# Forming the first pair's tokens already transposed, in a hybrid encoder kernel on one Trainium2 core

## The reference, cut to what matters

```python
def hier_moe(h, w_rg, b_rg, w_re, b_re, w_gate, w_up, w_down):
    t = h.reshape(B * S, D)
    ...                                   # group, two experts of it, weights
    for e in range(N_EXPERTS):            # 32
        he = jax.nn.silu(t @ w_gate[e]) * (t @ w_up[e])     # 1024 -> 256
        y = y + combine[:, e:e + 1] * (he @ w_down[e])      # 256 -> 1024
```

## Time and profile before

| | |
|---|---|
| median of 3 runs | 527.29 us (526.87 to 527.69) |
| profiled execution, span from first to last instruction | 526.4 us |
| profiled execution, its own time | not recorded apart from the span |
| PE busy | 491.7 us |
| PEld busy | 271.0 us |
| DVE, ACT, POOL busy | 212.8, 136.9, 75.1 us |
| packets of all DMAs | 139.95 MB, mean 266 GB/s |
| mean granted TensorE clock | 0.987 |

### The profile page before, as it was taken

One profiled execution on the slowest core, in us unless ns is written; L12 is line 12 of the kernel. 1 busy time (PEld: TensorE's weight loads), 2 busy tenths in 40 slices (PEclk: granted clock), 3 DMA queues, 4 the chain that ended last, 5 costly groups with the idle time before them and its releaser, 6 DMA issues.

```text
span 526.4 us, 7686 instructions
## 1 busy us (share of the span) xinstructions
PE 491.7 (93%) x2924; PEld 271.0 (51%) x2924; DVE 212.8 (40%) x565; ACT 136.9 (26%) x357; POOL 75.1 (14%) x101
## 2 busy tenths in 40 slices
PE   4999999999999999999999899999999978878894
PEld 4446544557765555455447555555555444444431
DVE  3317320666676671116763422223323312233167
ACT  3404211354476661203131111111111101112023
POOL 1000000361100000001113122222222222111000
PEclk9999999999999999999998999999999989999898
DMA  8996000010199004931089999999999999999984
GB/s 291 361 278 254 2 1 0 16 36 2 33 398 404 5 1 177 416 127 41 2 317 361 395 418 415 415 417 414 418 412 417 413 417 416 418 415 415 411 327 160
DMA packets 40134, 139.95 MB, mean 266 GB/s; under 512 B 9848, under 2 KB 12984, under 8 KB 31904
## 3 DMA queue, kind: packets, MB, share of 16 engines
q1 hardware_dynamic: 34752, 131.38, 63.5%
q0 software_dynamic: 4816, 7.85, 4.0%
q10 hardware_dynamic: 528, 0.22, 0.2%
HBM read 130.47 MB, written 16.39 MB: 279 GB/s over the span
## 4 chain that ended last, share of the span: by engine, by line
PE 65%; DMA 16%; SPq 9%; DVE 6%; issue 2%; ACT 1%; DVEq 0%; ACTq 0%; POOLq 0%
PE bank L747 12%; PE bank L1065 12%; DMA EW<-in_moe_w_up 9%; PE bank L933 9%; PE bank L1078 5%; SPq L615 5%; PE bank L906 5%; PE bank L976 3%; SPq L620 3%; PE bank L965 3%; DMA EW<-y_scratch 2%; PE bank L1038 2%; DMA EW<-in_w_in 2%; PE bank L755 1%; PE bank L853 1%
## 5 line engine op out<-in xcount | busy, mean ns | idle before, releaser
L1065 PE MATMUL bank<-EW,WO 128*64 128x256 f32 x640 | 78.5, 401 | 9.8 <-DMA EW<-in_moe_w_up 8.1
L1065 PEld LDWEIGHTS bank<-EW,WO 128*64 128x64 f32 x640 | 47.8, 144 | 35.6 <-DMA EW<-in_moe_w_up 9.8
L747 PE MATMUL bank<-EW,XT 128*128 128x512 f32 (+1 forms) x192 | 64.1, 495 | 0.0
L933 PE MATMUL bank<-WO,XT 128*128 128x512 f32 x128 | 56.6, 595 | 0.0
L1411 ACT ACTIVATE G<-bank 128x128 f32<-128x128 f32 x32 | 8.9, 277 | 178.9 <-PE bank L1065 178.9
L1778 DVE TENSOR_TENSOR G<-G,bank 128x128 f32<-128x128 f32 x32 | 9.2, 287 | 113.1 <-ACT G L1411 113.1
L2002 POOL DMA_INDIRECT y_scratch<-G,sidx x30 | 30.2, 1008 | 159.1 <-DVE G L1791 145.8
L747 PEld LDWEIGHTS bank<-EW,XT 128*128 128x128 f32 x192 | 32.9, 190 | 31.0 <-issue 31.0
L1791 DVE COPY G<-bank 128x512 f32<-128x512 f32 x32 | 22.1, 691 | 45.8 <-PE bank L1078 45.8
L1078 PE MATMUL bank<-EW,G 128*64 128x512 f32 x160 | 38.3, 599 | 0.0
L933 PEld LDWEIGHTS bank<-WO,XT 128*128 128x128 f32 x128 | 23.7, 190 | 27.3 <-issue 27.3
(11 more groups left out here) (295 smaller groups left out, 651.8 us busy)
## 6 DMA issues: line engine op xcount, KB each, us to landing
EW<-in_moe_w_gate SPq DMA_DIRECT2D x20, 1024.0 KB, 21.5
EW<-in_moe_w_up SPq DMA_DIRECT2D x20, 1024.0 KB, 21.4
EW<-in_moe_w_down SPq DMA_DIRECT2D x20, 1024.0 KB, 23.3
y_scratch<-MIX SPq DMA_DIRECT2D x8, 512.0 KB, 9.1
WO<-in_w_out SPq DMA_DIRECT2D x2, 2048.0 KB, 12.3
MIX<-in_moe_w_gate SPq DMA_DIRECT2D x4, 1024.0 KB, 20.6
MIX<-in_moe_w_up SPq DMA_DIRECT2D x4, 1024.0 KB, 22.6
WO<-in_moe_w_gate SPq DMA_DIRECT2D x4, 1024.0 KB, 19.7
```

The lines of the kernel that those rows point to most:

```text
L747: mm = pe.matmul(ps[:, 0:width], xnT[:, c, t * P:(t + 1) * P], w_in_sb[:, c, col:col + width], start=(c == 0), stop=(c == C - 1))
L933: mm = pe.matmul(ps[:, :], xnT[:, c, t * P:(t + 1) * P], w_out_sb[:, c, n * 512:(n + 1) * 512], start=(c == 0), stop=(c == C - 1))
L1065: mm = pe.matmul(bank[BLOCK * m:BLOCK * (m + 1), 0:2 * P].rearrange("p (w n) -> p w n", w=2), xeT[:, c, par * BLOCK:(par + 1) * BLOCK], wv ...
```

## The change

Pair 0's `pick` uses the rows of `X` as the stationary operand, in eight pieces of every eighth column, and `sel0` as the moving one, so that its products come out transposed, in the layout of the former transposes. For each t there are eight products with 128 columns, in place of two with 512. The copies to `xg[0]`, their semaphores and the eight transposes are gone: DVE and ACT copy from the banks to `xeT` with the gain as soon as bank 0 and bank 1 are complete. `pick_done` becomes `xe_full` 2 for SP and POOL. Pair 2's numbers move behind expert 0's `gate_up` on PE, and on DVE the weights of the last tile and `held_w` move ahead of pair 2's part.

```diff
-            sp.wait_ge(pick_done, 1)
+            sp.wait_ge(xe_full, 2)
...
-                    for n in range(2):
-                        mm = pe.matmul(banks[n][:, :], sel0[:, t].rearrange("p e s -> p (e s)"),
-                                       X[:, t, n * 512:(n + 1) * 512], start=(t == 0), stop=(t == T - 1))
-                    if t == T - 1:
-                        mm.then_inc(pick_done, 1)
+                    for c in range(C):
+                        mm = pe.matmul(banks[c // 4][:, c % 4 * P:(c % 4 + 1) * P], X[:, t, c:D:C],
+                                       sel0[:, t].rearrange("p e s -> p (e s)"), start=(t == 0 and c % 4 == 0),
+                                       stop=(t == T - 1), skip_group_check=True)
+                        if t == T - 1 and c % 4 == 3:
+                            mm.then_inc(xe_full, 1)
...
-            pe.wait_ge(sel4_ready, T)
-            for pair in (1, 2):
+            def token_numbers(pair):
...
-                if pair == 1:
-                    pe.wait_ge(picked, 2)
-                    for half in range(2):
-                        tokens(0, half).then_inc(xe_full, 1)
+
+            pe.wait_ge(sel4_ready, T)
+            token_numbers(1)
...
                 gate_up(place, par).then_inc(gu_full, 1)
                 if e == 0:
+                    token_numbers(2)
                     counts()
...
-            act.wait_ge(pick_done, 1)
-            act.wait_ge(x2_stored, 16 * T)
-            act.activation(xg[0][:, 512:D], banks[1][:, :], ACT.Copy).then_inc(picked, 1)
...
-            dve.wait_ge(pick_done, 1)
-            dve.wait_ge(x2_stored, 16 * T)
-            dve.tensor_copy(xg[0][:, 0:512], banks[0][:, :]).then_inc(picked, 1)
+            held_w = nm[:, 0:4 * T].rearrange("p (t e r) -> p t e r", e=2, r=2)
+            copy_tokens(0)
             for pair in (1, 2):
...
                 if pair == 1:
-                    copy_tokens(0)
-            link(weights(T - 1))
...
-            dve.tensor_tensor(held_w, oh[:, :, :, NE - 2:NE].rearrange("p t r e -> p t e r"),
-                              wts[:, :, :].unsqueeze(2).to_broadcast([P, T, 2, 2]), ALU.mult).then_inc(weights_ready, 1)
+                    link(weights(T - 1))
+                    dve.tensor_tensor(held_w, oh[:, :, :, NE - 2:NE].rearrange("p t r e -> p t e r"),
+                                      wts[:, :, :].unsqueeze(2).to_broadcast([P, T, 2, 2]), ALU.mult).then_inc(weights_ready, 1)
...
-                pool.wait_ge(*((pick_done, 1) if pair == 1 else (xe_full, 2 * pair - 2)))
+                pool.wait_ge(xe_full, max(2 * pair - 2, 2))
```

More of the change, by code:

```diff
@@ L464, in encoder_kernel @@
         xg_scaled = sem("xg_scaled")
-        pick_done = sem("pick_done")
-        picked = sem("picked")
         gu_landed = [sem(f"gu_landed{s}") for s in range(FIRST)]
@@ L1756, in _ @@
                 if pair == 1:
-                    copy_tokens(0)
-            link(weights(T - 1))
-            held_w = nm[:, 0:4 * T].rearrange("p (t e r) -> p t e r", e=2, r=2)
-            dve.tensor_tensor(held_w, oh[:, :, :, NE - 2:NE].rearrange("p t r e -> p t e r"),
-                              wts[:, :, :].unsqueeze(2).to_broadcast([P, T, 2, 2]), ALU.mult).then_inc(weights_ready, 1)
+                    link(weights(T - 1))
+                    dve.tensor_tensor(held_w, oh[:, :, :, NE - 2:NE].rearrange("p t r e -> p t e r"),
+                                      wts[:, :, :].unsqueeze(2).to_broadcast([P, T, 2, 2]), ALU.mult).then_inc(weights_ready, 1)
             def most():
```

## The result

| | before | after |
|---|---|---|
| median of the runs on one chip | 527.49 us (526.87 to 529.90) | 533.44 us (532.76 to 534.71) |
| ratio, 95% interval | 1 | 1.0104 (1.0081 to 1.0126) |
| profiled execution: span | 526.4 us | 531.6 us |
| its own time | not recorded | 533.38 us |
| mean granted clock | 0.987 | 0.986 |

The kernel became 1.0% slower where 0.3% faster was forecast. Own time and span lie 1.8 us apart here, so the span of before also stands for some 528.2 us, not for the median that the forecast set beside it.

What follows compares the result with a forecast made beforehand. A full DMA queue bounds the kernel from 300 us on; filling the thin stretch before wins 1.5 us, `pick`'s +0.13 costs nothing. Span 526.4 - 1.5 = 524.9, median 0.9 above: 525.8 us, own range 525.0 to 526.2.

Steps and rivals of the forecast that it cites:

- Part 1: `pick`: 16 products for each t at 0.122 us, 1.95 us together; +0.13 us in all, bounds 0 and +1.3.
- rival 4: Weight loads not hidden in the new `pick`: 0.225 us an instruction, `xe_full` 2 6.4 us later, 529.3 us; chance 0.04.
- hole: Thin DMA queue from 283 to 291 us, 318 GB/s against 416: 1.88 us to win.
- Part 2: Between `pick` and expert 0's `gate_up`: copies and transposes go, so `gate_up` starts at 278.87 us, 1.82 us earlier.
- Part 3: Clock at expert 0's `gate_up`: no fall, 3.67 us instead of 5.38, its products end 3.5 us earlier.
- rival 2: The clock falls all the same; expert 0's `gate_up` ends 1.8 us earlier, 526.3 us; chance 0.08.
- Parts 4 and 5: Pair 2's numbers behind expert 0's `gate_up`, gather covered; expert 7's loads 3.5 us earlier, later loads 1.7 us.
- The sum: Earlier loads close most of the hole: 1.5 us won, bounds 0.5 and 2.4, span 524.9 us.
- rival 1: No change that can be told: slow gather and scatter packets make the hole; gain 0.3 to 0.5, 526.9 us; chance 0.27.

Runs made afterwards that it cites:

- ladder: The kernel after, but `pick`'s pieces take columns of `X` with step 2, 1, 4 and 8 for t = 0 to 3; 529.34 us in one execution.
- contiguous: The kernel after, but `pick`'s pieces are 128 neighbouring columns of `X` (pair 0's features in another order); 528.9 us, ratio 1.0035.
- step_moving: The kernel before, but `X`, still `pick`'s moving operand, is read in pieces of every eighth column, 128 an instruction; 532.96 us in one execution.
- before_list: The kernel before with only the token list taken up one expert later; 527.79 us, ratio 0.9990.
- by_rows: `contig_warm`, with experts 0 and 1's gate and up rows and pair 0's gain in neighbouring-column order, to compute the reference; 527.95 us, ratio 1.0000.
- contig_warm: `contiguous` with three `keep_busy` products of 512 columns while PE waits for the list in expert 1; 527.43 us, ratio 0.9984.
- contig_warm_again: The same kernel as `contig_warm`, measured once more beside `by_rows`; 527.69 us, ratio 0.9995.
- contig_list: `contiguous` with the token list taken up one expert later; 527.65 us, ratio 1.0008.

## Why the prediction was wrong

**Part 1, the price of an instruction in `pick`, is the step that failed.** It took 0.122 us within 0.1125 and 0.145; it was 0.24 (7.86/32 = 0.246 with the tail in the kernel after, 3.81/16 = 0.238 for step 4 in `ladder`). The two rows that bounded it each lacked one half of the new form. Line 925 has real products, but neighbouring columns. The transposes of line 1038 have the step of eight, but each is one instruction, and they don't suffer from it: those of line 994 read `X` with the same step in the kernel after, and its rows stand against line 1019's 335 and 402 ns:

```profile
L994 PEld LDWEIGHTS bank<-ident,X x32: 185/192/254, 219.1 to 264.2; 128*128 128x128 f32 x32
L994 PE MATMUL bank<-ident,X x32: 272/274/348, 219.6 to 264.3; 128*128 128x128 f32 x32
```

`ladder`, `contiguous` and `step_moving` show the product with a step as its own case. The prediction bounded an operation that the trace didn't have, and put the upper end where the trace ended.

The Trainium skill, "Advanced Engine Details and Errata", Memory Cachelines, says that SBUF has lines of 16 bytes and that a read needs at least two hits on a line for full pace. `ladder` agrees: step 2 (two float32 values in 16 bytes) is free, step 4 (one) costs double. The transposes don't follow that rule. The forecast left this rule out. Weighed there, it would have given rival 4's time by another mechanism, and with it a larger chance.

**Rival 4 had the right end and the wrong cause.** It named an instruction price of 0.225, 6.4 us at `xe_full` 2, a dry queue and 529.3 us, at a chance of 0.04; measured were 0.24, 7.07 us, and 533.44. Its rule (a load that isn't hidden) falls to `contiguous`: the same loads at 0.119 an instruction. It was also sized too small. It won 2 us back from a closed hole, which couldn't be, since loads that go out later close nothing.

**Part 2 was right.** ACT's gain copies start straight behind `pick` (284.54, 1.14 us); in `contiguous` `gate_up` starts at 278.82, and 278.87 was forecast.

**Part 3 got its number, but not by its reason.** `gate_up` took 3.67 us in the kernel after and in `contiguous`. But `before_list` had the same 3.67 us with the old transposes and thin products ahead of it, and `ladder` 5.13 us, rival 2's case, with the change's order. The fall that part 3 meant to remove was that of one execution. So 1.7 of the 3.5 us by which expert 7's loads were to go out earlier was no gain of the change, and that "the clock fell behind transposes and thin products" holds for the profile read, not for the kernel.

**Parts 4 and 5 were right in `contiguous`, up to the list.** Expert 7's loads were forecast for 282.5 and went out at 282.53, place 5's weights for 279.4 (279.49), the list for 284.8 and landing at 291.7 (284.93 and 291.98). In `by_rows` the list came at 293.27.

**The sum had a second fault, which the price hid.** "From expert 2 on PE is thus 1.7 us ahead" needed an early list and a full clock. In `contiguous` the list wait became PE's idle time, the clock fell behind it, and expert 9's loads came later than before; in `by_rows` the list came at the old time. But even where they did come earlier, by 1.4 and 1.0 us (`contig_warm`, `contig_warm_again`), 3.0 us (`before_list`) and 4.0 us (`contig_list`), the ratios are 0.9984, 0.9995, 0.9990 and 1.0008. The sum took a filled hole for time won. In `contiguous` and `by_rows` a later stretch lost part of the bytes again. In the others the lead was gone by the last expert but one (488.57 to 489.00 against 488.69), `contig_warm`'s first profile excepted; where they lost it stays open. So even with the right price, the change is worth nothing that can be measured: 1.0000 (0.9983 to 1.0018), rival 1's outcome, though not through its cause, since the hole did fill.

## What to carry to other kernels

Before an operand gets a new access pattern, look for a row with the same step and the same kind of instruction (a product, not a transpose); if there is none, the bounds must reach to at least twice the price, and the doubt belongs into the chances. Where the end is set by a full transfer queue, follow each load to the next one behind it, up to the last: a filled hole can reappear later, and here even loads that went out 3 to 4 us earlier bought nothing that could be measured. Removing work ahead of a wait of another engine can turn into idle time, and that may be followed by a lower clock. Before a clock fall is counted as something to win, look whether it is there in a second execution of the same code.

## What was not expected of the hardware

- A float32 product of 128x128 with 128 columns takes 0.12 us an instruction with a step of 1 or 2 values and 0.24 with 4 or 8, on the stationary and on the moving side alike; transposes of the same operand with step 8 stay at 274 ns beside 402. Why they differ stays open.
- ACT's copy of 128x1024 float32 values with a step of eight on the read side took 2.04 us.
- PE idle for 2.17 us was followed by a clock of 0.50 over 6 us (`contiguous`); with six 512-column products in its place the clock was 1.00 in all three profiles.
- The same instructions behind the same wait ran at full clock in one execution and at half in another: 3.67 against 5.36 us at expert 0 (`before_list`, kernel before), and again near the end, behind some 2 us of waiting, in four profiles against five.
- Two profiled executions of one kernel lay 2.5 us apart in span (524.2 and 526.7): 1.95 us in when a matrix arrived near the end, 1.1 of these from one early stretch of loads, and some 0.55 us in the clock.
